# Where a decoder step's output copies are issued: three sequences' cache copies of each layer leave the search stage

## The chip, the cores and the metric

One core of a Trainium2 chip runs the whole kernel as one program. The metric is device time in microseconds (us) for one execution; lower is better. The engines that appear are TensorE (PE in the rows, its weight loads PEld), the vector engine (DVE), the scalar engine (ACT), GpSimd (POOL) and SyncE (SP). SyncE and GpSimd issue the transfers; all transfers run on the core's 16 DMA engines.

## The reference, cut to what matters

One inference step of a two-layer decoder trunk in float32: 256 prompt tokens and 8 sequences with 4 new tokens each, model width 1024.

```python
def layer_sample(x, pool_kv, pool_ki, layer, page_table, dil_bufs, conv_state, ssd_state, prm):
    (q_a, k_a, v_a, g_a, qi, ki, wi, q_c, k_c, v_c, g_c, z, xbc, dt_raw) = mixer_inputs(x, norm_w, w_in, pos)
    o_a = dsa_sample(q_a, k_a, v_a, qi, wi, ki, pool_kv, pool_ki, layer, page_table)
    o_c, new_bufs = dilated_sample(q_c, k_c, v_c, dil_bufs)
    y_b, conv_new, h_new = ssd_branch(z, xbc, dt_raw, conv_state, ssd_state, ...)
    y = x + merge_out(o_a, g_a, o_c, g_c, y_b, w_out)

def dilated_sample(q, k_new, v_new, bufs):
    for buf, kn, vn in zip(bufs, split_groups(k_new), split_groups(v_new)):
        kk = jnp.concatenate([buf[:, :, 0], kn], axis=1)
        vv = jnp.concatenate([buf[:, :, 1], vn], axis=1)
        new_bufs.append(jnp.stack([kk[:, t_new:], vv[:, t_new:]], axis=2))
```

A layer normalises x, multiplies it with one input matrix, runs three branches (sparse attention over 2048 cached tokens, of which the best 256 by an index score are kept for each query; dilated window attention with windows of 128, 512 and 2048 tokens; a state-space branch) and adds the output product to x. Part of the result are the window caches `new_bufs`: the old cache of each sequence and group, shifted by four tokens, with the new ones at the end. The shifted part is only copied, from one DRAM tensor to another.

## The kernel before, in words

**Tiles.** All activations lie with features on partitions and 288 tokens (256 + 32) in the free dimension. The input matrix is cut into 35 tiles of 128 columns (`proj0` to `proj34`), the output matrix into 8 (`out0` to `out7`). Every tile is 8 matmuls of 128x128 by 128x288 in float32 and needs one weight tile of [128, 8, 128] floats. TensorE's helper `mm` (L825) writes nearly every matmul, `turn` (L875) the transposes.

**Stages of a layer, in TensorE's order.** The front: proj0 to proj7. The page stage: 16 pairs of cache pages for index scores and key products, with proj8 to proj15 between them. The search stage: proj16 to proj26, one or three counting matmuls in each, because the vector engine finds each query's 256th score bit by bit (31 steps of compare at L1453, count on TensorE, settle at L1464 and L1466). Then window keys, masks, the softmax, and the value stage with proj27 to proj34, in which pages of values and windows are read. Last the output tiles: out0, out1 and out2 are begun with parts that are ready early and end close together; out3 to out7 follow whole. After out2 and each tile behind it comes one matmul with ones that sums the squares of the next norm.

**Weights.** The tile `w` has four slots (WSLOTS = 4). SyncE loads the weights of a tile into the slot of the tile four places before, once that tile's last matmul is done: `next_w(i)` waits for `filled(proj i)` or `filled(out m)` and calls `load_w` (issue L425). The order runs on from out7 of layer 0 to proj0 of layer 1.

**Pages.** `kv` has eight slots. RING lists 74 items a layer in the order of their use: 32 key pages, 8 + 8 windows and 32 groups of values. `consumed(items)` calls `after`, which issues the load of the item eight places later, SyncE the even ones and GpSimd the odd ones (`load_item`, issues L397 and L404); each waits until the slot has been read. So in the last value groups of layer 0 the first eight key pages of layer 1 are already loaded.

**Copies.** `keep(b, use)` makes GpSimd wait for `filled(use)`, and then issues three DRAM-to-DRAM copies for sequence b of layer L (L496), one for each group: (window - 4) rows of 256 floats. There are 16 calls. In both layers they stand in GpSimd's program after proj16, 17, 18, 19, 20, 21, 23 and 24:

```python
def keep(b, use):
    pool.wait_ge(filled(use), nth(L, use))
    for g in range(3):
        pool.dma_start(a[f"keep{g}"][ly, b], a[f"buf{g}"][ly, b, 4 * 256:]).then_inc(S["copied"], 16)
```

Nothing but GpSimd's very last instruction waits for `copied`.

**GpSimd's order in a layer.** The odd page loads of the page stage; a memset of `qcz`; the conv tails; copies, feature outputs (`feat`, L500), masked state inputs (`masked`, L518) and the placing of the window queries (L539, L543), mixed by hand in the search stage; the odd loads of windows and values, with the state output between; the value features; the last page loads; then waits for all outputs of the layer except the copies. Every wait holds up what stands behind it. SyncE's order is `next_w` and `consumed` alone, and one load of the old states after the page stage.

Of the kernel before, what the change touches and what calls it, by code (L numbers as in the profile page):

```python
# [57 lines left out]
def slot_of(i):  # L58

    first = max(f for f in SLOTS if f <= i)  # L60
    return SLOTS[first] + i - first
# [43 lines left out]
def ring_counts():  # L105

    used, landed, total, n = [], [], [0] * NKV, 0
    for at, (kind, i) in enumerate(RING):
        end = f"ks{i // 8}" if kind == "page" and i // 2 % 4 == 3 else {("window", NB - 1): "dk", ("window", 2 * NB - 1): "do",
                                                                           ("value", NGRP - 1): "so"}.get((kind, i))  # L110
        n += 0 if end else i % 2 if kind == "page" else 1
        used.append((end, None) if end else ("kv_used", n + 1 - i % 2 if kind == "page" else n))
        total[at % NKV] += 16 if kind == "window" else 64
        landed.append(total[at % NKV])
    return used, landed, total, n


USED, LANDED, LANDED_ALL, KV_USED = ring_counts()


def chunk_of(u):
# [88 lines left out]
def build(nc, a):  # L210

    plan, _ = bank_plan()
    with ExitStack() as ctx:
# [103 lines left out]
        def filled(use):  # L317
            return S[f"filled{plan[use][0]}"]
# [4 lines left out]
        def nth(layer, what, n=None):  # L323

            if n is None:
                what, n = f"filled{plan[what][0]}", plan[what][1] + 1
            return layer * PER[what] + n
# [15 lines left out]
        def C(name, lo=0, hi=None, rows=slice(0, P)):  # L343
            o, wd = _C[name]
            return const[rows, o + lo:o + (wd if hi is None else hi)]
# [9 lines left out]
        def ptile(i, lo=0, hi=T, rows=slice(0, P)):  # L355
            return pt[rows, slot_of(i), lo:hi]
# [30 lines left out]
        def load_item(engine, kind, layer, at):  # L387


            if layer or at >= NKV:  # L390
                what, n = USED[at - NKV]
                l = layer if at >= NKV else layer - 1
                engine.wait_ge(S[what] if n else filled(what), nth(l, what, n))
            s = at % NKV
            what, item = RING[at]
            if what == "window":
                engine.dma_start(kv[:, s, 0:9 * P], a["dil"][layer, item]).then_inc(S[f"kv_in{s}"], 16)  # L397
                return
            rec, entry = (KREC, 4 * item) if what == "page" else (VREC, 4 * (KITEMS + item))
            pages = nc.values_load_multi_w_load_instructions(  # L400
                ptab[0:1, entry:entry + 4], engines=[kind], min_val=0, max_val=N_POOL - 1,
                skip_runtime_bounds_check_because="a page table names pages of the pool")[1]
            for r, page in enumerate(pages):
                engine.dma_start(kv[:, s, r * rec:(r + 1) * rec],  # L404
                                 a["kk" if what == "page" else "vv"][bass.ds(page + layer * N_POOL, 1)].rearrange("o p n -> (o p) n")
                                 ).then_inc(S[f"kv_in{s}"], 16)

        def after(engine, kind, layer, item):


            at = PLACE[item] + NKV
            layer, at = (layer, at) if at < len(RING) else (layer + 1, at - len(RING))
            if layer < DEPTH and at % 2 == (kind == mybir.EngineType.Pool):
                load_item(engine, kind, layer, at)
# [67 lines left out]
        @block.gpsimd  # L482
        def _(pool):
            POOL = mybir.EngineType.Pool
            pool.wait_ge(S["ptab_in"], 16)
            for i, item in enumerate((1, 3, 5, 7)):
                pool.wait_ge(filled(f"proj{i}"), nth(0, f"proj{i}"))
                load_item(pool, POOL, 0, item)
            for L in range(DEPTH):
                ly = bass.ds(L, 1)  # L490
# [7 lines that stand above are left out]
                def feat(lo, hi, o, landed_out="feat_out"):  # L498

                    pool.dma_start(a["feat"][ly, :, o:o + hi - lo, :].rearrange("o p a n -> (o p) a n"),  # L500
                                   pt[:, slot_of(lo):slot_of(lo) + hi - lo, :]).then_inc(S[landed_out], 16)

                def consumed(*items):

                    for item in items:
                        after(pool, POOL, L, item)

                for u in range(NPAIR):
                    consumed(("page", 2 * u), ("page", 2 * u + 1))
                    if u == 3:  # L510
                        pool.memset(qcz, 0.0).then_inc(S["qcz_zero"], 1)
                pool.wait_ge(S["conved"], nth(L, "conved", NXBC))
                pool.dma_start(a["tails"][ly].rearrange("o p a n -> (o p) a n"), tails[:, :, :]).then_inc(S["tail_out"], 16)
                def masked(b):

                    if b >= 2:
                        pool.wait_ge(filled(f"ss{b - 2}"), nth(L, f"ss{b - 2}"))
                    pool.tensor_scalar(xwb[:, b % 2, :], xws[0:32, 2, :], C("bm", b, b + 1, slice(0, 32)), None,  # L518
                                       ALU.mult).then_inc(S["xwb_ready"], 1)

                keep(0, "proj16")
                pool.wait_ge(S["roped"], nth(L, "roped", 9))
                feat(KI, KI + 1, 0, "ki_out")
                feat(KA, KA + 2, 1)
                keep(1, "proj17")
                keep(2, "proj18")
                pool.wait_ge(S["xws_ready"], nth(L, "xws_ready", 1))
                masked(0)
                masked(1)
                keep(3, "proj19")  # L530
                keep(4, "proj20")
                keep(5, "proj21")
                pool.wait_ge(S["roped"], nth(L, "roped", 12))
                pool.wait_ge(S["qcz_zero"], nth(L, "qcz_zero", 1))
                for g in range(3):
                    for h2 in range(2):
                        q = ptile(QC + g, TP, T, half(h2)).rearrange("p (b q) -> p b q", q=NQ)
                        place = qcz[half(h2), :].rearrange("p (g b q n) -> p g b q n", g=3, b=NB, n=32)[:, g, :, :, QCZ0 + h2]
                        pool.tensor_copy(place, q).then_inc(S["qcz_ready"], 1)  # L539
                for g in range(3):  # L540
                    for h2 in range(2):
                        q = ptile(QC + g, TP, T, half(h2)).rearrange("p (b q) -> p b q", q=NQ)
                        pool.tensor_copy(qcbd[half(h2), g, :, h2:2 * NB:2], q.rearrange("p b q -> p q b")).then_inc(S["qcbd_ready"], 1)  # L543
                keep(6, "proj23")
                keep(7, "proj24")
                consumed(*RING[32:40])
                pool.wait_ge(S["roped"], nth(L, "roped", 15))
                feat(KC, KC + 3, 5)
                masked(2)
                masked(3)  # L550
                consumed(*RING[40:44])
                masked(4)
                masked(5)
                consumed(*RING[44:46])
                masked(6)
                masked(7)
                consumed(*RING[46:54])
                pool.wait_ge(drained(f"ss{NB - 1}"), nth(L, f"ss{NB - 1}"))
                pool.dma_start(a["s_ssd"][ly].rearrange("o p a n -> (o p) a n"), state[:, :, :]).then_inc(S["h_out"], 16)
                pool.dma_start(a["p_ssd"][ly].rearrange("o p n -> (o p) n"), hfin[:, :]).then_inc(S["h_out"], 16)  # L560
                consumed(*RING[54:66])
                pool.wait_ge(drained(f"proj{VA + 1}"), nth(L, f"proj{VA + 1}"))
                feat(VA, VA + 2, 3)
                feat(VC, VC + 3, 8)
                consumed(*RING[66:])
                for name in ("ki_out", "feat_out", "tail_out", "h_out"):
                    pool.wait_ge(S[name], nth(L, name, PER[name]))
            pool.wait_ge(S["copied"], DEPTH * PER["copied"])
# [1623 lines left out]
```

## Time and profile before

| what | us |
|---|---|
| median of 3 runs | 673.66 |
| lowest and highest of them | 668.64 and 677.35 |
| the profiled execution's own time | 673.8 |
| its span, first to last instruction | 672.1 |
| TensorE busy | 611.9 (91%) |
| vector engine busy | 377.8 (56%) |
| GpSimd busy | 224.0 (33%) |
| scalar engine busy | 168.1 (25%) |

The core's DMA engines moved 198.38 MB, a mean of 295 GB/s; a DRAM-to-DRAM copy is counted once in it. The stages in this execution: search of layer 0 from 112 to 202 us, its output tiles from 303 to 334 us, front of layer 1 to 367 us, its page stage to 427 us, its search to 524 us, its output tiles from 629 to 660 us. In the rows a busy digit is tenths of a slice; "to landing" is the time from a transfer's issue to its semaphore.

### The profile page before, as it was taken

The page shows a single profiled execution, that of the slowest core. Times are in us where ns is not written, and L with a number is a line of the kernel's source. Part 1 is how long each engine was busy: PE and PEld are TensorE (multiplying, and loading weights), DVE is VectorE, ACT ScalarE, POOL GpSimd, SP SyncE. Part 2 cuts the span into 40 slices and gives each one's busy share as a digit, 9 for nine tenths or more (in the row PEclk, how much of TensorE's full clock was granted, in tenths as well). Part 3 has the DMA queues.
Part 4 walks back from the last instruction along what each step waited for, and adds up shares of the span by engine and source line. Part 5 has one row for each costly group of instructions (what it writes and reads, how often), then busy time and mean ns, then how long its engine had stood idle before and what let it go on. Part 6 is the DMA issues. An engine that isn't in the chain of part 4 may idle for free.

```text
span 672.1 us, 13786 instructions
## 1 busy us (share of the span) xinstructions
PE 611.9 (91%) x4870; PEld 426.9 (64%) x4870; DVE 377.8 (56%) x1150; ACT 168.1 (25%) x405; POOL 224.0 (33%) x406
## 2 busy tenths in 40 slices
PE   5999998888899989999999999988888989789994
PEld 3766564665567665667776656566665867556772
DVE  3765565677569545443167475577756855343413
ACT  3024222121113312451101433212201151126211
POOL 0507530241206676451000664124120377642000
PEclk9999999898889998999999999999878999889998
DMA  7979999999968989996334999999997598996031
GB/s 294 308 274 356 368 369 413 417 358 331 353 236 262 314 305 369 366 329 234 110 121 134 323 368 369 402 413 355 349 394 265 181 333 287 374 357 214 10 118 70
DMA packets 67766, 198.38 MB, mean 295 GB/s; under 512 B 11537, under 2 KB 40370, under 8 KB 66418
## 3 DMA queue, kind: packets, MB, share of 16 engines
q1 hardware_dynamic: 49682, 99.99, 42.8%
q0 software_dynamic: 18016, 97.50, 40.3%
q8 instruction: 39, 0.64, 0.4%
q14 instruction: 29, 0.24, 0.1%
HBM read 189.30 MB, written 52.00 MB: 359 GB/s over the span
## 4 chain that ended last, share of the span: by engine, by line
PE 63%; DVE 15%; DMA 13%; ACT 4%; issue 2%; SPq 2%; DVEq 0%; ACTq 0%
PE bank L825 60%; DMA w<-in_w 5%; DMA kv<-in_vv 4%; DMA kv<-in_kk 4%; DVE hit L1453 3%; PE bank L875 3%; SPq L404 2%; DVE tb L1466 1%; DVE st L1955 1%; ACT srow L766 1%; ACT shared L663 1%; DVE tb L1464 1%; DMA x<-in_x 1%; DVE shared L1576 1%; ACT shared L680 1%
## 5 line engine op out<-in xcount | busy, mean ns | idle before, releaser
L825 PE MATMUL bank<-xn,w 128*128 128x288 f32 x1120 | 307.0, 429 | 0.7 <-DMA w<-in_w 0.7
L825 PEld LDWEIGHTS bank<-xn,w 128*128 128x128 f32 x1120 | 213.9, 198 | 74.9 <-issue 19.1
L404 POOL DMA_DIRECT2D kv<-in_vv x160 | 86.3, 539 | 96.9 <-PE bank L825 69.5
L404 POOL DMA_DIRECT2D kv<-in_kk x128 | 68.8, 538 | 144.5 <-issue 96.1
L616 ACT ACTIVATE pt<-bank 128x288 f32<-128x288 f32 x48 | 19.6, 409 | 243.4 <-PE bank L825 243.4
L825 PE MATMUL bank<-pt,w 128*128 128x288 f32 x256 | 64.9, 407 | 0.0
L825 PEld LDWEIGHTS bank<-pt,w 128*128 128x128 f32 x256 | 48.3, 190 | 13.6 <-issue 0.8
L496 POOL DMA_DIRECT2D out_keep<-in_buf x48 | 23.5, 495 | 85.1 <-PE bank L825 78.7
L1453 DVE TENSOR_SCALAR_CACHE_REDUCE hit<-sc,tb 128x516 bf16<-128x516 f32 x62 | 46.5, 750 | 2.2
L825 PE MATMUL bank<-kv,pt 128*32 128x256 f32 x512 | 37.5, 404 | 11.0 <-DMA kv<-in_vv 10.7
L1464 DVE TENSOR_SCALAR tb<-bank 128x1 int32<-128x1 f32 x62 | 9.5, 153 | 48.7 <-PE bank L825 48.5
L825 PE MATMUL bank<-kv,qz 128*32 128x256 f32 x512 | 34.3, 385 | 0.0
L2022 DVE TENSOR_TENSOR x<-x,bank 128x288 f32<-128x288 f32 x16 | 7.3, 455 | 43.6 <-PE bank L825 43.3
L825 PEld LDWEIGHTS bank<-cnt,seg 128*128 128x128 f16 x68 | 6.9, 103 | 38.8 <-issue 36.7
L825 PE MATMUL bank<-cnt,seg 128*128 128x1 f16 x68 | 11.2, 169 | 21.8 <-DVE hit L1453 21.1
L1426 DVE COPY tails<-cin 128x3 f32<-128x3 f32 x14 | 7.2, 512 | 41.0 <-ACT cin L614 38.9
L825 PEld LDWEIGHTS bank<-kv,pt 128*32 128x32 f32 x512 | 14.1, 112 | 22.5 <-DMA kv<-in_vv 9.5
L825 PE MATMUL bank<-kv,shared 128*32 128x128 f32 x768 | 26.8, 285 | 0.0
L825 PE MATMUL bank<-pt 64*128 64x128 f32 (+3 forms) x168 | 26.3, 334 | 0.0
L518 POOL TENSOR_SCALAR xwb<-xws,const 32x384 f32<-32x384 f32 x16 | 21.2, 1329 | 13.4 <-DVE xws L1716 7.7
L583 ACT ACTIVATE phased<-x 128x288 f32<-128x288 f32 x24 | 10.5, 442 | 60.0 <-DVE x L2022 57.1
L825 PEld LDWEIGHTS bank<-pt 64*128 64x128 f32 (+2 forms) x168 | 17.9, 183 | 10.6 <-issue 9.8
(238 smaller groups left out, 796.7 us busy)
## 6 DMA issues: line engine op xcount, KB each, us to landing
w<-in_w SPq DMA_DIRECT2D x86, 512.0 KB, 7.3
out_keep<-in_buf POOLq DMA_DIRECT2D x16, 2044.0 KB, 13.0
kv<-in_kk SPq DMA_DIRECT2D x128, 160.0 KB, 8.2
kv<-in_kk POOLq DMA_DIRECT2D x128, 160.0 KB, 5.8
kv<-in_vv POOLq DMA_DIRECT2D x160, 128.0 KB, 5.6
kv<-in_dil SPq DMA_DIRECT2D x24, 576.0 KB, 7.5
kv<-in_vv SPq DMA_DIRECT2D x96, 128.0 KB, 7.3
out_keep<-in_buf POOLq DMA_DIRECT2D x16, 508.0 KB, 8.5
```

The source lines that it names most:

```text
L404: engine.dma_start(kv[:, s, r * rec:(r + 1) * rec], a["kk" if what == "page" else "vv"][bass.ds(page + layer * N_POOL, 1)].rearrange("o p ...
L496: pool.dma_start(a[f"keep{g}"][ly, b], a[f"buf{g}"][ly, b, 4 * 256:]).then_inc(S["copied"], 16)
L518: pool.tensor_scalar(xwb[:, b % 2, :], xws[0:32, 2, :], C("bm", b, b + 1, slice(0, 32)), None, ALU.mult).then_inc(S["xwb_ready"], 1)
L583: act.activation(squares[:, k % 2, 0:T], x[:, k, :], ACT.Square).then_inc(S["sq_ready"], 1)
L616: act.activation(ptile(i), src[:, 0:T], fn).then_inc(use, 1)
L663: act.activation(psa[:, i, 0:nk], psa[:, i, 0:nk], ACT.Exp, bias=st8[:, 1, i:i + 1], accum_out=st8[:, 2, i:i + 1]).then_inc(S["pexp"] if i ...
L825: return pe.matmul(out, lhsT, rhs, start=start, stop=stop, skip_group_check=True, **k)
L875: return pe.transpose(out, in_, ident(n))
L1426: dve.tensor_copy(tails[:, n, 0:3], cin[:, n % 2, TP:TP + 3]).then_inc(chain.next(), 1)
L1453: ts_(hit[:, :], sc[:, :], old.bitcast(F32), 0.0, ALU.is_ge, ALU.add, accum_out=cnt[:, 0:1]).then_inc(S["cnt_ready"], 1)
L1464: ts_(tb[:, 2:3], src[:, 0:1], float(TOPK_S), float(bit), ALU.is_lt, ALU.mult).then_inc(drained(f"count{n}"), 1)
L2022: tt_(x[:, m, :], x[:, m, :], src[:, 0:T], ALU.add).then_inc(drained(f"out{m}"), 1)
```

## The change

Before, the calls stood one by one in GpSimd's program; now three tables say which sequence is copied where. The search stage keeps five calls a layer, after proj16, 17, 19, 21 and 23. In layer 0 they carry sequences 0 to 4, and sequences 5, 6 and 7 are copied after out0, out3 and out6. In layer 1 sequences 0 and 1 are copied after proj1 and proj5, ahead of the page loads in GpSimd's program, sequences 2 to 6 in the search stage, and sequence 7 after out0. The number of copies, their sizes and their destinations stay. No other engine's program changes.

```diff
@@ -116,6 +116,11 @@
 
 
 USED, LANDED, LANDED_ALL, KV_USED = ring_counts()
+
+
+FRONT_KEEPS = ((), ((0, "proj1"), (1, "proj5")))
+STAGE_KEEPS = ((0, 1, 2, 3, 4), (2, 3, 4, 5, 6))
+OUTPUT_KEEPS = (((5, "out0"), (6, "out3"), (7, "out6")), ((7, "out0"),))
 
 
 def chunk_of(u):
@@ -505,6 +510,8 @@
                     for item in items:
                         after(pool, POOL, L, item)
 
+                for b, use in FRONT_KEEPS[L]:
+                    keep(b, use)
                 for u in range(NPAIR):
                     consumed(("page", 2 * u), ("page", 2 * u + 1))
                     if u == 3:
@@ -518,18 +525,16 @@
                     pool.tensor_scalar(xwb[:, b % 2, :], xws[0:32, 2, :], C("bm", b, b + 1, slice(0, 32)), None,
                                        ALU.mult).then_inc(S["xwb_ready"], 1)
 
-                keep(0, "proj16")
+                keep(STAGE_KEEPS[L][0], "proj16")
                 pool.wait_ge(S["roped"], nth(L, "roped", 9))
                 feat(KI, KI + 1, 0, "ki_out")
                 feat(KA, KA + 2, 1)
-                keep(1, "proj17")
-                keep(2, "proj18")
+                keep(STAGE_KEEPS[L][1], "proj17")
                 pool.wait_ge(S["xws_ready"], nth(L, "xws_ready", 1))
                 masked(0)
                 masked(1)
-                keep(3, "proj19")
-                keep(4, "proj20")
-                keep(5, "proj21")
+                keep(STAGE_KEEPS[L][2], "proj19")
+                keep(STAGE_KEEPS[L][3], "proj21")
                 pool.wait_ge(S["roped"], nth(L, "roped", 12))
                 pool.wait_ge(S["qcz_zero"], nth(L, "qcz_zero", 1))
                 for g in range(3):
@@ -541,8 +546,7 @@
                     for h2 in range(2):
                         q = ptile(QC + g, TP, T, half(h2)).rearrange("p (b q) -> p b q", q=NQ)
                         pool.tensor_copy(qcbd[half(h2), g, :, h2:2 * NB:2], q.rearrange("p b q -> p q b")).then_inc(S["qcbd_ready"], 1)
-                keep(6, "proj23")
-                keep(7, "proj24")
+                keep(STAGE_KEEPS[L][4], "proj23")
                 consumed(*RING[32:40])
                 pool.wait_ge(S["roped"], nth(L, "roped", 15))
                 feat(KC, KC + 3, 5)
@@ -563,6 +567,8 @@
                 feat(VA, VA + 2, 3)
                 feat(VC, VC + 3, 8)
                 consumed(*RING[66:])
+                for b, use in OUTPUT_KEEPS[L]:
+                    keep(b, use)
                 for name in ("ki_out", "feat_out", "tail_out", "h_out"):
                     pool.wait_ge(S[name], nth(L, name, PER[name]))
             pool.wait_ge(S["copied"], DEPTH * PER["copied"])
```

## Rows read from the trace of the kernel before

**Rows 1.** The page's 40 slices of 16.8 us, whole run.

```profile
PE   5999998888899989999999999988888989789994
...
DMA  7979999999968989996334999999997598996031
```

**Rows 2.** Waits of PE: engine, line, released by: us, times, longest.

```profile
PE bank L825 <- DVE hit L1453: 21.1, 20, 1.7
PE bank L825 <- DMA kv<-in_vv: 10.7, 8, 2.6
...
PE bank L825 <- DMA w<-in_w: 0.7, 1, 0.7
```

**Rows 3.** Stretches: us, busy time by engine, PEclk, DMA share, GB/s.

```profile
112.00:202.00 90.00, 78.91 (x430) 55.63 (x425) 60.65 (x229) 15.29 (x45) 18.27 (x40) 0.91 0.93 343
303.00:322.00 19.00, 19.00 (x92) 14.72 (x91) 5.78 (x17) 2.21 (x6) 1.32 (x3) 1.00 0.58 202
322.00:359.00 37.00, 37.00 (x154) 28.74 (x153) 19.40 (x49) 4.49 (x10) 0.00 (x0) 1.00 0.39 128
```

**Rows 4.** DMA issues: form, count, KB each, median us to landing.

```profile
w<-in_w SPq DMA_DIRECT2D x86, 512.0 KB, 7.3
out_keep<-in_buf POOLq DMA_DIRECT2D x16, 2044.0 KB, 13.0
...
out_keep<-in_buf POOLq DMA_DIRECT2D x16, 508.0 KB, 8.5
...
out_keep<-in_buf POOLq DMA_DIRECT2D x16, 124.0 KB, 6.7
```

**Rows 5.** GpSimd's copies: issue time in ns, span of starts, landing.

```profile
L496 POOL DMA_DIRECT2D out_keep<-in_buf x48: 486/497/532, 117.7 to 505.9; - x48
...
DMA to landing us min/median/max: 4.7/10.9/24.5
```

**Rows 6.** Landing of proj24's weights: layer 0 (issued 147.1), then layer 1.

```profile
DMA to landing us min/median/max: 23.9/23.9/23.9
...
L425 SPq DMA_DIRECT2D w<-in_w x1: 328/328/328, 467.9 to 467.9; - x1
...
DMA to landing us min/median/max: 30.9/30.9/30.9
```

**Rows 7.** DMA queues in 475:485: packets, MB, share.

```profile
q0 software_dynamic: 116, 3.00, 83.4%
q1 hardware_dynamic: 115, 0.41, 13.5%
```

**Rows 8.** Weight loads issued in 310:313, layer 0's output tiles.

```profile
L425 SPq DMA_DIRECT2D w<-in_w x3: 328/338/339, 310.5 to 312.4; - x3
...
DMA to landing us min/median/max: 3.4/5.7/6.0
```

**Rows 9.** Timeline of PE in 317:331: start, us, tile's matmuls.

```profile
317.07 4.04 PE L825 MATMUL bank<-pt,w 128*128 128x288 f32 x16
...
321.43 4.04 PE L825 MATMUL bank<-pt,w 128*128 128x288 f32 x16
...
325.80 4.04 PE L825 MATMUL bank<-pt,w 128*128 128x288 f32 x16
```

**Rows 10.** Landing of GpSimd's first value load, issued at 205.9.

```profile
DMA to landing us min/median/max: 2.5/2.7/2.9
```

**Rows 11.** Stretches in which PE waited for value pages.

```profile
249.00:254.00 5.00, 1.87 (x38) 1.17 (x40) 0.00 (x0) 0.00 (x0) 4.37 (x9) 0.85 1.01 344
...
575.00:580.00 5.00, 2.94 (x44) 1.78 (x40) 0.00 (x0) 0.00 (x0) 3.40 (x7) 0.68 1.07 401
```

**Rows 12.** Weight loads issued in 636:640, layer 1's output tiles.

```profile
L425 SPq DMA_DIRECT2D w<-in_w x3: 328/328/339, 636.7 to 638.7; - x3
```

**Rows 13.** Weight loads in 343:359.2; SyncE's first page load of layer 1.

```profile
L425 SPq DMA_DIRECT2D w<-in_w x5: 328/328/328, 343.4 to 359.0; - x5
...
370.27 0.88 SPq L404 DMA_DIRECT2D kv<-in_kk  x2
```

## The prediction

> **What bounds the kernel now.** I read the slices first [rows 1]: TensorE is at 8 or 9 tenths almost everywhere, and the DMA row is also at 9 except in two hollows, slices 20 to 23 (from the end of layer 0 into the front of layer 1) and the last four. So the matmuls set the time, and the transfers are close behind. Then TensorE's waits [rows 2]: 21.1 us for the vector engine's hits in the search, 10.7 us for value pages, and for weights one wait of 0.7 us in the whole run. Then the stretches that the change touches [rows 3]: the search stage of layer 0 (112 to 202 us) has a DMA share of 0.93 and a granted clock of 0.91; the output tiles and the next front (303 to 359 us) have 0.58 and 0.39, and TensorE is busy for all 56 us. The search therefore has little DMA time left and TensorE is often idle there; the output stretch has much DMA time left and TensorE never idle. What is moved is 3 of 8 copies per layer from the first to the second.
>
> **What one copy weighs.** keep(b) issues three DRAM-to-DRAM copies of 2044, 508 and 124 KB [rows 4], 2676 KB or 2.74 MB. A weight tile is 512 KB, 0.524 MB [rows 4]. All 48 are issued between 117.7 and 505.9 us, 0.5 us of GpSimd each, and take 4.7 to 24.5 us to land [rows 5].
>
> **Part 1: search stage, copies taken out.** The issue costs GpSimd 1.5 us a copy. The whole of it lies in GpSimd's own waits; nothing on TensorE's path reads it. The visible price of the copies is the late weight tile. The one issued at 467.9 us needs 30.9 us to land [rows 6]; it is the cause of the 0.7 us wait of [rows 2]. By the code six copies stand around it, one after each of proj16 to proj21, each 2.74 MB or some 8 us of DMA, and the tile is proj24's. With five copies spread over proj16, 17, 19, 21 and 23 the pile is gone: gain 0.7 us. Bounds: 0, and 5 us if the loads are later in other executions than in this one; I take 0.7, what the row shows. The vector engine's waits and the clock of 0.91 come from the search's chain, which no copy feeds, so I count nothing there. The copy after proj24 disappears, but the value loads begin only once the search is over, at 205.9 us, and land in 2.5 to 2.9 us [rows 10], on idle DMA, so it gives nothing. The other transfers of GpSimd in the stage (features, masks, the query copies) keep their order and their later waits.
>
> **Part 2: how a weight load fares beside a copy.** In 475 to 485 us only copies and weight loads move [rows 7]: queue 0 (GpSimd's) passed 116 packets with 3.00 MB, queue 1 (SyncE's) 115 packets with 0.41 MB. They alternate packet for packet, and a copy's packets are seven times as large. One weight tile is 0.524 MB, so beside a copy it takes 0.524/0.041, about 12.8 us; alone it takes 3.4 us [rows 8]. In the search nobody minds: 11 projections share 90 us, some 8 us each, and four slots give about 30. An output tile lasts 4.04 us plus the norm's matmul, 4.37 us from one to the next [rows 9], and four slots are gone in 13.
>
> The Trainium skill ("DMA: Bandwidth & Descriptors", SWDGE vs HWDGE vs iDMA) says the engine changes queue at packet borders and that a packet is preferably at most 4096 B. Equal packets would share the bandwidth evenly and no weight would be late. The trace shows 3.6 KB a packet on SyncE's queue and 26 KB on GpSimd's, so for these copies I go by the row; the page's case is rival B.
>
> **Part 3: layer 0, copies after out0, out3 and out6.** out0 ends at 310.5 us and out3 at 316.8 us, because the first three output tiles end almost together (weights are requested at 310.5, 311.4 and 312.4) [rows 8]. So copy 5 and copy 6 start only 6.3 us apart, and each needs 2.74/0.36 = 7.6 us alone: they run back to back. Walk through the weights:
> - out4's tile is requested at 310.5 us, at the same moment as copy 5. It lands after 3.4 us and is needed at 317.1 [rows 8, 9]. GpSimd's transfers land at the earliest 2.5 us after issue [rows 10], so the copy begins when most of the tile has passed: 0, bounds 0 to 3 us.
> - out5's tile (needed at 321.4) and out6's (needed at 325.8) queue behind it, beside both copies. From 311.6 us, when the tile starts, two copies and three tiles must pass: 2 x 2.74 + 3 x 0.524 = 7.05 MB. At 0.369 MB/us (343 GB/s at a share of 0.93 [rows 3]) that ends at 330.7 us, at 0.341 MB/us [rows 7] at 332.3 us. Three tiles have more packets than two copies, so the last tile is the last to land: out6 starts at 331 to 332.3, 5.2 to 6.5 us late. I take 5.8. Bounds: 0 (the tiles pass first) and 10 (out4's tile is caught behind a large packet and out5's then waits for both copies).
> - After TensorE idles for 2 to 3 us in 5, the clock is granted at 0.68 and 0.85 of full [rows 11]. At 0.68, 64% of the 5 us are at 1.2 GHz: 1.6 us lost. I add 1.6 us once; bounds 0 and 3.2.
> - copy 7 after out6 is alone. The tile requested with it is ahead of it, the next is 12 us under way and needed after 17. Nothing.
>
> **Part 4: layer 1, copies after proj1 and proj5.** proj1 ends at 343.4 us, proj5 at 359.0 [rows 13]; the copies are 15.6 us apart, so each is alone, and by the same walk each tile is in time by 3 us or more. GpSimd waits for proj1 and proj5 with its page loads queued behind, but their slots are freed by the first page pair; SyncE's first is issued at 370.3 us [rows 13]. At the start of the front it has nothing else to do. Copy 1, issued at 359, ends near 371 us; the first page load after it fills a slot of an eight-slot ring whose other six slots, three pairs of some 3.7 us, are still to be read (16 pairs lie in the 60 us from 367 to 427), so it is needed near 381. Cost 0, bounds 0 to 2 us.
>
> **Part 5: layer 1, copy 7 after out0.** Three tiles are requested between 636.7 and 638.7 us [rows 12]. One copy and two tiles are 3.79 MB, 10.3 us from 637.9: 648.2 us, and out5 wants its tile 10.9 us after out0's end, as in layer 0, at 647.6. I take 1 us with the completion, bounds 0 and 3. GpSimd's last wait, for all copies, ends near 650, with 22 us to the end as cover.
>
> **Sum.** On the profiled execution, 673.8 us around a span of 672.1 and beside a median of 673.66: minus 0.7, plus 5.8, plus 1.6, plus 1.0 is plus 7.7, **681.5 us**.
>
> **Rivals.**
> A is the forecast: two copies back to back hold up the output weights of layer 0. 678 to 686 us, chance 0.50.
> B: the weights pass. SyncE's descriptors might be ready earlier than GpSimd's, and the share packet for packet may hold only while both queues are full. For it: the tile of 310.5 us lands before the copy starts. Against it: [rows 7]. 673.8 - 0.7 = 673.1 us; with one small wait, 675. Chance 0.27.
> C: more of it. out4's tile is caught by a large packet in both layers, and out5's waits behind both copies: 10 + 3.2 (two clock drops) + 3 (layer 1) + 1 (front) - 0.7 = 16.5, 690 us. Chance 0.13.
> D, on the other side: the late weights of the search are the main thing. In layer 0 the same tile took 23.9 us, in layer 1 30.9 [rows 6]; TensorE can stand about 30. An execution with a slightly slower DMA pays that lateness on each tile of the pile, 4 to 5 us, and the executions shown go from 668.64 to 677.35. If removing it gives 5 us and the output stretch costs nothing, 669 us. It decides where more than two tiles of the search are late; here one is. Chance 0.10.
> That GpSimd reaches the new places late, and the copies are not moved at all in effect, I exclude: behind its last page loads for layer 1, which wait for the value groups and not for an output tile, nothing keeps it from those waits.
>
> **Range and chances.** Two per cent, 13.5 us, is about what a measurement of this kernel can tell from no change. Below 660.2 us lies only an unknown cause: 0.02. Above 687.1 lies C: 0.13. Within: 0.85. The range of 670 to 688 us holds A and B whole and leaves out half of D and most of C. A alone has 678 to 686.
>
> **What would show it.** Right: a wait of TensorE for weights of 5 to 7 us between 317 and 333 us, out6's first matmul near 331.5, weight loads of 10 to 18 us to landing there against 3.4 to 6.0, a slice with a clock below 1.0 in the output tiles, and in the search weight loads below 20 us with no wait. Wrong: no wait for weights there (B); a first matmul of out4 after 318 us (C); a search stage shorter by more than 2 us (D). A longer page stage in layer 1 would break part 4.

## The result, and the profile after

| | before | after |
|---|---|---|
| median of the runs, us | 674.07 (4 runs) | 686.97 (4 runs) |
| lowest and highest | 668.64 and 677.35 | 685.61 and 688.84 |
| the profiled execution's span | 672.1 | 685.7 |

The change makes the kernel slower: the ratio is 1.0202, with a 95% interval of 1.0151 to 1.0253. The forecast was 681.5 us, plus 7.7; it came to plus 12.9. Here and below the medians hold every run, while a ratio and its interval leave out the runs more than 1.5% above the fastest of the same kernel.

The page of the changed kernel, in 40 slices of 17.1 us; the first and third line answer to [rows 1]:

```profile
PE   5999998989999979997999989988889998899974
...
PEclk9999999999899989999999999999988999899998
DMA  7879999976639899999798999999751788994331
```

The DMA row's hollow after layer 0 is filled, and new ones lie in the search of layer 0 (slices 10 to 12) and of layer 1 (slices 29 to 31). PE's 7 in slice 19 (309 to 326 us) is new, and so is the 7 in slice 39 (651 to 669 us). In those two slices and just behind them lies most of the loss. TensorE's waits, which answer to [rows 2]:

```profile
PE bank L831 <- DVE hit L1459: 19.7, 20, 1.7
PE bank L831 <- DMA kv<-in_vv: 10.8, 7, 2.5
PE bank L831 <- DMA w<-in_w: 9.3, 3, 4.0
...
PE bank L831 <- DMA kv<-in_kk: 4.2, 5, 1.5
```

The vector engine's and the value pages' waits are as before (19.7 against 21.1, and 10.8 against 10.7). The weights have gone from 0.7 to 9.3 us in three waits, and the key pages from 2.6 to 4.2. All weight waits stand in output tiles. The three loads requested after out0, out1 and out2 of layer 0, where [rows 8] had 3.4 to 6.0 us:

```profile
L430 SPq DMA_DIRECT2D w<-in_w x3: 328/339/339, 310.0 to 311.9; - x3
...
  PE bank L831: 5.5, 2
...
DMA to landing us min/median/max: 3.6/14.1/21.0
```

The middle line says what TensorE waited for them. In the timeline of PE, which answers to [rows 9], out4, out5 and the beginning of out6:

```profile
316.58 4.04 PE L831 MATMUL bank<-pt,w 128*128 128x288 f32 x16
...
325.09 5.84 PE L831 MATMUL bank<-pt,w 128*128 128x288 f32 x16 [3.98 <-DMA w<-in_w]
...
332.95 4.15 PE L831 MATMUL bank<-pt,w 128*128 128x288 f32 x16 [1.53 <-DMA w<-in_w]
```

out4 starts as before. out5's weights come at 325.1 us, 14.1 us after their request, and out6's at 332.9, after 21.0. The forecast had out4 on time and out6 between 331 and 332.3. out5 is also slower in itself, 5.84 us against 4.04. The stretches behind the two long waits, with the granted clock in the third column from the end, answer to [rows 11]:

```profile
322.00:326.00 4.00, 0.91 (x3) 0.72 (x4) 0.00 (x0) 0.00 (x0) 0.00 (x0) 0.95 1.13 359
326.00:330.00 4.00, 4.00 (x11) 2.90 (x11) 0.00 (x0) 0.00 (x0) 0.00 (x0) 0.63 0.82 290
655.00:660.00 5.00, 1.23 (x6) 0.67 (x5) 0.46 (x1) 0.44 (x1) 0.00 (x0) 1.00 0.67 240
660.00:665.00 5.00, 5.00 (x16) 3.60 (x15) 0.00 (x0) 0.00 (x0) 0.00 (x0) 0.66 0.02 9
```

After TensorE worked 0.91 of 4 us, the clock is granted at 0.63 in the next 4; after 1.23 of 5 us in layer 1, at 0.66. That is the second price beside the wait itself: out5's matmuls run mostly at 1.2 GHz and take 1.8 us longer. In layer 0 it isn't paid on top, because out6's weights come only at 332.9 us, after out5 has ended. In layer 1 out6's weights are there in time, and it is paid. The tiles requested in layer 1 after out1 and out2, where copy 7 starts with out0:

```profile
L430 SPq DMA_DIRECT2D w<-in_w x2: 328/328/328, 645.6 to 646.5; - x2
...
  PE bank L831: 3.8, 1
...
DMA to landing us min/median/max: 13.9/14.0/14.2
```

Where the 13.6 us between the two spans came from follows from five marks in both timelines (first and last addition to x of a layer's outputs, the new keys' dots that open the page stage, the scores that close it, the selection of value sums ahead of the outputs):

| stretch | before | after | difference |
|---|---|---|---|
| start to the first output of layer 0 | 310.5 | 310.0 | -0.5 |
| output tiles of layer 0 and front of layer 1 | 57.5 | 65.3 | +7.8 |
| page stage of layer 1 | 67.0 | 68.4 | +1.4 |
| search and value stage of layer 1 | 194.3 | 193.4 | -0.9 |
| output tiles of layer 1, to the last addition | 31.2 | 37.0 | +5.8 |
| the rest | 11.6 | 11.6 | 0.0 |

How far each line can be trusted is seen from the same marks in the profiles of the experiments below. Wherever no weights were late, the second line is 57.5 or 57.6 us and the fifth 31.2 or 31.3, so +7.8 and +5.8 are the change's. The first line goes from 306.2 to 316.6 us and the fourth from 187.8 to 194.6 without any order by placement, so -0.5 and -0.9 say nothing.

In the search the copies' going did what was said of it, and no more: layer 1's weight loads there landed in 5.6 to 30.9 us before; now it is

```profile
L430 SPq DMA_DIRECT2D w<-in_w x10: 327/328/912, 448.6 to 523.0; - x10
...
DMA to landing us min/median/max: 3.4/4.5/13.1
```

and no wait for them is left. The search stretch of layer 0, which answers to the first line of [rows 3]:

```profile
112.00:202.00 90.00, 80.25 (x486) 56.86 (x486) 62.90 (x234) 16.59 (x47) 13.93 (x31) 0.92 0.71 260
```

The DMA share is 0.71 in place of 0.93, the clock 0.92 in place of 0.91. From its scores to the first maximum of the softmax the search of layer 0 took 96.2 us against 99.1, and that of layer 1 99.3 against 99.9. The 2.9 us in layer 0 look like the sign that the prediction gave for rival D, but they go with the clock of that execution (last section) and not with the copies: experiment 2, which leaves layer 0's copies where they were, has 97.7 us there. What was freed there was of no use that can be shown.

### The profile page after: what moved, and what is told of

Read it like the earlier page. It is cut to its first block, busy times and chain, and to the rows that moved or that the text cites. A ratio compares the mean times of both kernels' runs of the same rounds, so it can differ in the third digit from the quotient of the medians.

```text
span 685.7 us, 13786 instructions
## 1 busy us (share of the span) xinstructions
PE 617.2 (90%) x4870; PEld 429.8 (63%) x4870; DVE 376.7 (55%) x1150; ACT 168.4 (25%) x405; POOL 224.3 (33%) x406
## 2 busy tenths in 40 slices
DMA packets 67766, 198.38 MB, mean 289 GB/s; under 512 B 11537, under 2 KB 40370, under 8 KB 66418
## 3 DMA queue, kind: packets, MB, share of 16 engines
q0 software_dynamic: 18016, 97.50, 39.4%
## 4 chain that ended last, share of the span: by engine, by line
PE 59%; DVE 16%; DMA 16%; ACT 4%; issue 3%; SPq 2%; DVEq 0%; ACTq 0%
PE bank L831 56%; DMA kv<-in_kk 6%; DMA w<-in_w 5%; DMA kv<-in_vv 4%; DVE hit L1459 4%; PE bank L881 3%; SPq L409 2%; DVE tb L1472 1%; DVE tb L1470 1%; DVE st L1961 1%; ACT srow L772 1%; ACT shared L669 1%; DMA x<-in_x 1%; DVE shared L1582 1%; ACT shared L686 1%
## 5 line engine op out<-in xcount | busy, mean ns | idle before, releaser
L831 PE MATMUL bank<-pt,w 128*128 128x288 f32 x256 | 68.6, 424 | 9.3 <-DMA w<-in_w 9.3
L831 PEld LDWEIGHTS bank<-pt,w 128*128 128x128 f32 x256 | 50.2, 199 | 25.2 <-DMA w<-in_w 10.7
L831 PE MATMUL bank<-kv,pt 128*32 128x256 f32 x512 | 37.1, 400 | 11.1 <-DMA kv<-in_vv 10.8
L831 PE MATMUL bank<-cnt,seg 128*128 128x1 f16 x68 | 11.2, 169 | 20.4 <-DVE hit L1459 19.7
L589 ACT ACTIVATE phased<-x 128x288 f32<-128x288 f32 x24 | 10.5, 442 | 73.8 <-DVE x L2028 70.6
```

The lines of the kernel that those rows point to most:

```text
L589: act.activation(squares[:, k % 2, 0:T], x[:, k, :], ACT.Square).then_inc(S["sq_ready"], 1)
L831: return pe.matmul(out, lhsT, rhs, start=start, stop=stop, skip_group_check=True, **k)
```

## The experiments

Each kernel was timed against the kernel before on the same chip; "before" below is that comparison's own median. The edits are given against the kernel before, shortened to what they do. `stage_keep(use)` issues the copy that a table names for this place, and none where the table has no entry.

**1. Layer 0's part alone.**

```diff
+STAGE_KEEPS layer 0: proj16, 17, 19, 21, 23 -> sequences 0 to 4
+OUTPUT_KEEPS layer 0: (5, "out0"), (6, "out3"), (7, "out6")
 layer 1: as before
```

> Layer 0 as in the change (copies after proj16, 17, 19, 21, 23 and after out0, out3, out6), layer 1 as before. Theory 1 (two copies back to back take the DMA time of the weights of out5 and out6): TensorE waits for weights 5 to 6 us in layer 0's output tiles, out5's matmuls run partly at the lower clock, and nothing else changes: 6 to 8 us above before, 680 to 682 us. Rival (the copies in the front and after layer 1's out0 cost the most, or the whole program is shifted by something general): under 3 us above before.

Measured: 683.38 us against 672.99, ratio 1.0154 (1.0072 to 1.0237). The mechanism is there, the median is larger than expected (four runs; the interval reaches from 4.8 to 16 us). The timeline of PE, out4, out5 and out6:

```profile
318.54 4.04 PE L839 MATMUL bank<-pt,w 128*128 128x288 f32 x16
...
329.43 5.53 PE L839 MATMUL bank<-pt,w 128*128 128x288 f32 x16 [6.36 <-DMA w<-in_w]
...
335.28 4.04 PE L839 MATMUL bank<-pt,w 128*128 128x288 f32 x16
```

Here out5's weights come 6.4 us late and out6 then finds its own in place. This is another order of the same walk: out5's tile lands at 329.4 us, 5.4 us after the first copy's large part and 4.2 us before the second's. The forecast's upper bound (10 us) was for out5 behind both copies. The stretch of output tiles and next front took 65.5 us, 8.0 more than before, so the order hardly changes the price. The profile has another 3.1 us of waits for weights in the search of layer 1, whose copies stand at the old places (loads there landed in up to 36.1 us, and the waits were 2.7 and 0.4 us). That belongs to the kernel before as well, which had 0.7 us of it in its own profile.

**2. The front alone.** Sequences 0 and 1 of layer 1.

```diff
+FRONT_KEEPS layer 1: (0, "proj1"), (1, "proj5")
-keep(0, "proj16"), keep(1, "proj17") in layer 1
```

> Only layer 1's copies 0 and 1 are moved, to proj1 and proj5 of its front; all else as before. Theory 1 (single copies with a tile's distance around them cost nothing in the front): 0 to 2 us above before, all of it in the page stage behind the copy at proj5. Rival (each moved copy costs the same, 13 us over 6 copies): 4 to 5 us above before.

Measured: 673.4 us against 672.99, ratio 1.0029 (0.9982 to 1.0076). Copies with a tile's distance to the requests cost little. The interval, up to 5.1 us, doesn't quite exclude the rival of an equal price for each copy (4 to 5 us); the profile does: output tiles and front took 57.6 us against 57.5, the page stage behind them 67.9 against 67.0. There seems to be a small price: the page stage of layer 1 takes 67.9, 68.4, 68.5, 69.1 and 69.4 us in the five kernels that issue a copy after proj5, and 66.4 to 67.7 in the eight that don't. These are single executions. Layer 0's page stage, which no copy precedes in any kernel, takes 67.0 to 67.9 us in twelve of them and 71.8 in experiment 11, whose 69.4 is therefore a weak witness. About 1 us is what is left. The changed kernel's last part of that copy, 2044 KB:

```profile
L501 POOL DMA_DIRECT2D out_keep<-in_buf x1: 497/497/497, 368.9 to 368.9; - x1
...
DMA to landing us min/median/max: 11.1/11.1/11.1
```

GpSimd issues it at 368.9, 2.4 us behind the copy's first part, and it lands at 380.0. That is 13.5 us after the first issue, where I had 12. The pages that GpSimd loads from 378 us on are behind it.

**3. Layer 1's copy 7 alone.**

```diff
+OUTPUT_KEEPS layer 1: (7, "out0")
-keep(7, "proj24") in layer 1
```

> Only layer 1's copy 7 is moved, to out0; all else as before. Theory 1 (the tile of out5 waits behind the one copy, then the clock drops): one wait for weights of 3.5 to 4.5 us and 1.8 us of slower matmuls, 5 to 6 us above before. Rival (the wait in the changed kernel came from its late start or from chance): under 2 us.

Measured: 677.37 us against 672.99, ratio 1.0072 (1.0035 to 1.0108). The weight loads after out0, out1 and out2 of layer 1:

```profile
L430 SPq DMA_DIRECT2D w<-in_w x3: 328/328/338, 636.3 to 638.2; - x3
...
  PE bank L839: 1.4, 1
...
DMA to landing us min/median/max: 3.7/11.5/13.5
```

The profiled execution had a wait of 1.4 us, less than the changed kernel's 3.8, no slower tile behind it, and output tiles 1.7 us longer than before; the ten timed ones lose 4.4 in the median. The 3.5 to 4.5 us of waiting and 1.8 us of slower matmuls that I expected are not in this profile. So one copy has a price of its own, and it varies.

**4. Rows of 4096 bytes, the first attempt.**

```diff
-pool.dma_start(new, old)
+for lo, hi in ((0, n - n % 16), (n - n % 16, n)):     # n rows of 4096 bytes
+    pool.dma_start(new rows lo:hi as [rows, 1024], old rows lo:hi as [rows, 1024])
```

> All copies where the change puts them, but each is issued as rows of 4096 bytes (a part with a multiple of 16 rows and the rest of it), so that the packets of both queues are alike; twice as many issues on GpSimd. Theory 1 (a weight load is late because the DMA engines alternate packet for packet and a copy's packets are many times larger): weight loads land in 4 to 8 us beside a copy, no wait for weights over 1 us, 672 to 676 us. Rival (a copy's bytes alone fill the DMA, whatever their packets): waits for weights of 9 us as in the changed kernel, 685 to 688 us.

Measured: 677.61 us against 672.99, ratio 1.011 (1.0008 to 1.0212). The page's count of packets, and two of the issue groups:

```profile
DMA packets 69304, 198.39 MB, mean 293 GB/s; under 512 B 12306, under 2 KB 41139, under 8 KB 67955
...
out_keep<-in_buf POOLq DMA_DIRECT2D x16, 1984.0 KB, 9.4
...
out_keep<-in_buf POOLq DMA_DIRECT2D x48, 60.0 KB, 6.4
```

This is a miss as a test. The kernel before has 67766 packets, this one 69304, 1536 of them from GpSimd's queue. The kernel before issues 48 parts and this one 96, so each further issue brought 32 packets, 16 of them below 512 bytes (12306 against 11537). Rows of 4096 bytes would be over 600 packets a copy: rows that lie one behind the other were joined to long packets again. What had changed is only when the parts are issued. GpSimd paused after the second of the six issues and began the 1984 KB part about 3.7 us after the first part (the changed kernel's large part starts after 1.0 us), out5 and out6 had their weights in time, and two waits of 1.4 and 1.0 us came in the front, a third of 1.0 us in layer 1's output tiles. That pointed to the moment of the large packets as the thing to test, besides their size.

**5 and 6. Rows of 4096 bytes, 8192 apart.** The large parts go as two interleaved sets of rows, which can't be joined; in 5 at the places of the change, in 6 at those of before.

```diff
+for t in range(2):                                    # the first 480 (or 96) rows
+    pool.dma_start(rows t, t + 2, t + 4, ... of new, the same rows of old)
+pool.dma_start(the rest of new, the rest of old)
```

> All copies where the change puts them, but the large parts are issued as two interleaved sets of rows of 4096 bytes, rows 8192 bytes apart, so that a packet can't hold more than one row (contiguous rows had been joined again in the kernel before this one). Theory 1 (alternating packet for packet with large packets makes the weights late): the two queues' packets are alike, weight loads land in 4 to 8 us beside a copy, no wait for weights over 1 us, 672 to 675 us. Rival (the copy's bytes fill the DMA, whatever the packets): 9 us of waits as in the changed kernel, 684 us and more.

Measured: 675.25 us against 672.63, ratio 1.0047 (1.0008 to 1.0086). No wait for weights is left. The loads after out0, out1 and out2 of layer 0, and the two queues from 312 to 322 us, beside copy 5:

```profile
L430 SPq DMA_DIRECT2D w<-in_w x3: 328/338/338, 309.2 to 311.2; - x3
...
DMA to landing us min/median/max: 3.5/7.9/10.0
```

```profile
q0 software_dynamic: 455, 1.64, 50.8%
q1 hardware_dynamic: 389, 1.45, 41.0%
```

In the changed kernel the same stretch, 313 to 323 us, has

```profile
q0 software_dynamic: 147, 3.32, 87.3%
q1 hardware_dynamic: 161, 0.61, 16.5%
```

The bytes of a copy are the same, and a load beside it takes 7.9 to 10.0 us in place of 14.1 to 21.0. Where both queues are full and the packets alike (3.6 KB and 3.7 KB), they share 455 to 389. So the size of the packets, not the bytes, made the weights late, and the rival falls. One thing differs besides: with seven issues a copy, the large rows start 2.5 us after out4's request and not 1.2. That can't make the two queues share alike once both are at work, but it may be part of why no wait is left. 2.6 us are left; the page stage of layer 1 has 1.5 of them (68.5 us against 67.0).

> The kernel before with the same rows of 4096 bytes in its copies. Theory 1: the weight loads of the search stage land in under 12 us in place of 10 to 31, the one wait of 0.7 us is gone, and nothing else gains: 670 to 674 us, no difference from before. Rival (the late weights of the search cost several us in most executions): 668 us or less. Small packets might also make the copies themselves longer; if they spill into the value loads, 675 us and more.

Measured: 673.55 us against 672.63, ratio 1.0021 (0.998 to 1.0062). The search's weight loads land in 6.4 to 9.1 us in layer 1, where they had 5.6 to 30.9, and it gains nothing: the late weights of the search cost nothing that the medians can show. Here the copies start where they did before, so the shorter landing is the packets' doing.

**7. Output copies after out3 and out6.**

```diff
+STAGE_KEEPS layer 0: proj16, 17, 18, 19, 21 -> 0 to 4, proj23 -> 7
+OUTPUT_KEEPS layer 0: (5, "out3"), (6, "out6")
```

> Layer 0's copies 5 and 6 after out3 and out6, copy 7 back in the search after proj23 and copy 5's old place left empty; layer 1 as before. Theory 1 (out0 is the bad place, because out4, out5 and out6 are requested within 2 us there and a second copy follows before the first is done): no wait for weights, or one under 1.5 us, 672 to 676 us. Rival (any copy between output tiles makes weights late): 4 us or more for each of the two, 681 us and more.

Measured: 673.4 us against 672.63, ratio 1.0026 (0.9978 to 1.0073), and no wait for weights; output tiles and front take 57.5 us, as before. Two copies in the output tiles, with weights landing in 9.7 and 9.3 us beside them, cost nothing that shows when the requests are 4.4 us apart and the copies 13 (the interval reaches up to 4.9 us).

**8. No copies.**

```diff
-pool.dma_start(a[f"keep{g}"][ly, b], a[f"buf{g}"][ly, b, 4 * 256:]).then_inc(S["copied"], 16)
```

> The kernel before without its 48 copies; the shifted part of the window caches isn't written. It bounds what any placement can give. Theory 1 (the search stage pays 0.7 us for its copies): 671 to 673 us, the search stages no more than 1 us shorter. Rival (the copies slow the search by several us through late weights or otherwise): 667 us or less, with both search stages shorter by 2 us or more.

Measured: 674.07 us against 672.63, ratio 0.9995 (0.9954 to 1.0035). The search of layer 0 and the weight loads of layer 1's:

```profile
112.00:202.00 90.00, 78.87 (x426) 55.12 (x423) 59.37 (x224) 16.00 (x45) 6.63 (x16) 0.91 0.29 103
```

```profile
L430 SPq DMA_DIRECT2D w<-in_w x11: 327/328/328, 438.2 to 518.6; - x11
...
DMA to landing us min/median/max: 3.3/3.5/7.0
```

With a third of its DMA share (0.29 for 0.93) and weights in 3.5 us, TensorE is busy for 78.87 us of the 90, before it was 78.91, and the search of layer 0 took 99.3 us against 99.1 at the same clock of 0.91. In the old places the copies were free within the interval's 0.5%, some 3 us, so no placement of them could have won more than that. The kernel without copies also leaves out the last wait, for `copied`.

**9. One copy after out0 in layer 0.**

```diff
+STAGE_KEEPS layer 0: proj16, 17, 18, 19, 21, 23 -> 0, 1, 6, 2, 3, 4
+OUTPUT_KEEPS layer 0: (5, "out0"), (7, "out6")
```

> Layer 0's copies 5 and 7 after out0 and out6, copy 6 back in the search (after proj18); layer 1 as before. Against a_l0_outputs it takes away the second of the two copies that follow each other. Theory 1 (out5's and out6's weights wait for both copies): the weights wait only behind one, so 1.5 to 4 us of waits and up to 1.8 us for the clock: 675 to 678 us, half of a_l0_outputs' loss or less. Rival (the loss comes from one copy after out0, the second adds nothing): 680 us and more.

Measured: median 678.58 us against 673.75, ratio 1.0031 (0.9989 to 1.0073), but the ten runs go from 670.26 to 685.45. As a size this is inconclusive. The profiled execution, with 680.42 us one of the long ones, is read for its order alone: one wait, for out5, and out6 finds its weights:

```profile
319.10 4.04 PE L839 MATMUL bank<-pt,w 128*128 128x288 f32 x16
...
326.90 4.15 PE L839 MATMUL bank<-pt,w 128*128 128x288 f32 x16 [3.27 <-DMA w<-in_w]
```

out5's tile takes 4.15 us after this wait, and 1.00 is granted in 326 to 331 us: the lower clock didn't follow here.

**10. Layer 1's copy 7, 1.9 us later.**

```diff
+OUTPUT_KEEPS layer 1: (7, "out2")
```

> As c_l1_out0, but layer 1's copy 7 starts after out2 in place of out0, 1.9 us later, when the weights of out4, out5 and out6 are all requested. Theory 1 (what counts is how many packets of the weights are ahead of the copy's): out5's tile is through before the copy's large packets come, no wait for weights over 0.5 us, within 1.5 us of before. Rival (a copy anywhere in the output tiles costs the same): 4 us above before, as c_l1_out0.

Measured: 672.63 us against 673.75, ratio 0.998 (0.9942 to 1.0017); against experiment 3 the whole loss is gone. The copy's issue and the three weight loads:

```profile
633.87 1.49 POOL L501 DMA_DIRECT2D out_keep<-in_buf  x3 [23.21 <-PE bank L839]
```

```profile
L430 SPq DMA_DIRECT2D w<-in_w x3: 327/328/338, 631.7 to 633.6; - x3
...
DMA to landing us min/median/max: 3.5/4.6/5.9
```

The three loads are requested from 631.7 to 633.6 us, the copy at 633.9. They land in 3.5 to 5.9 us, as in [rows 8].

**11. The change, shifted.**

```diff
+STAGE_KEEPS layer 0: proj16, 17, 18, 19, 21 -> 0 to 4, proj23 -> 7; layer 1: as in the change
+OUTPUT_KEEPS: layer 0 (5, "out2"), (6, "out5"); layer 1 (7, "out2")
+FRONT_KEEPS layer 1: (0, "proj1"), (1, "proj5")
```

> The change with its output copies shifted: layer 0's copies 5 and 6 after out2 and out5 (13 us apart), its copy 7 left in the search after proj23, layer 1's copies 0 and 1 after proj1 and proj5 as in the change, its copy 7 after out2. Theory 1 (the loss is the moment of the copies against the weight requests, not their place in the output and front stretches): no wait for weights over 1 us in any output tile, 672 to 676 us, 11 us or more below the change. Rival (five copies outside the search cost what the change costs, wherever they start): 681 us and more. Since the kernel without any copies isn't faster than before, neither theory has it below 671 in the median.

Measured: 675.94 us against 672.31, ratio 1.0069 (1.0033 to 1.0105). No wait for weights; TensorE's waits for pages:

```profile
PE bank L839 <- DMA kv<-in_vv: 10.2, 6, 3.0
...
PE bank L839 <- DMA kv<-in_kk: 5.5, 3, 2.7
```

The median is 11 us below the change's, and the loss against the kernel before on the same chip went from 12.9 to 3.6 us, by moving three starts by 2 to 9 us and leaving one copy in the search. Output tiles and front are back at 57.5 us, and layer 1's output tiles at 31.2. Of the 3.6 us some 1 us may be the copy after proj5 (experiment 2); for the rest there is no run. The rows above don't name it: 3.3 of the 5.5 us for key pages lie in layer 0's page stage, ahead of every copy.

## Why the prediction was right or wrong

**What bounds the kernel, and part 1.** Right. The stall of 0.7 us went, nothing else did that can be told from the spread. One reading was careless: the hollow of the DMA row is slices 19 to 22, and slices 12, 31 and 32 are low as well (6, 7 and 5); nothing in the sum uses it. The bound of 5 us that I kept for part 1 (rival D) is refuted by experiments 6 and 8: without late weights, and even without copies, the median stays. Single executions can pay more than 0.7, as the 3.1 us in experiment 1's profile show. The executions of before differ by 9 us for another reason, below.

**Part 2, the alternation.** Right in what it does, shown by experiment 5 against the changed kernel. The page of the Trainium skill ("DMA: Bandwidth & Descriptors", SWDGE vs HWDGE vs iDMA) gives 4096 bytes as the packet that is preferred; with such packets its case (rival B) is what happens, no late weights. The copies as written have other packets, and the trace of before had said so. [rows 7] had 116 packets against 115; the changed kernel has 147 against 161 in 313 to 323 us, and with alike packets it is 455 to 389.

**Part 3, layer 0.** Right in the mechanism; that the sum fits so well is partly luck. Forecast 5.8 + 1.6 = 7.4 us, measured 7.8 in the profile; out4 in time, out6 at 332.95. But out6 alone started 7.65 us late (22.95 us after out0's end in place of 15.3), and the slower matmuls of out5, which I had added on top, passed while out6's weights were still under way. So one term was 1.9 us too small and the other cost nothing extra. The walk had three tiles beside the two copies, 7.05 MB; from 311.6 to 332.9 us 7.62 MB passed, since the tiles requested after out3 and out4 were in the queue too. The order of out5 and out6 is not fixed: in experiment 1 out5 had the whole wait. There the stretch lost 8.0 us, so either order costs about the same.

**Part 4, the front.** Nearly right: no late weights in the front, but 1.4 us in the page stage, where I had 0 with a bound of 2. Copy 1 was issued 7.5 us later than in my walk, because of layer 0's loss, and took 13.5 us in place of 12. I had left out that GpSimd's issue can itself be held up, here by 1.4 us between two parts (by what, the profile doesn't show), and the large part took 11.1 us to land from its own issue.

**Part 5, layer 1's copy 7.** This is the term that failed, by its size. I took 1.0 us (bound 3); it measured 5.8 in the profile, and in experiment 3, where it stands alone, 4.4 in the median (2.4 to 7.3) and 1.7 in the profile. Two things were missing. The first is bytes. The tile of out5 landed 13.9 us after its request, when I had 10.5. I let one copy and two tiles pass, 3.79 MB. From 645.8 us to 659.5, when the tile landed, the two queues passed

```profile
q0 software_dynamic: 112, 2.74, 51.8%
q1 hardware_dynamic: 537, 1.96, 39.2%
```

which is the copy and nearly four tiles: out4's, of which 0.04 MB had passed before, and out7's, requested at 650.9 us, are in it. They passed at 344 GB/s, where I had 369 at a full share; most of the error is the 0.9 MB. How little of the weights gets through beside the copy's large part is plainest in 650 to 655 us, packet for packet:

```profile
q0 software_dynamic: 27, 1.50, 74.3%
q1 hardware_dynamic: 28, 0.10, 5.0%
```

The second is the clock. I charged it only in layer 0, though a like wait is followed by it in layer 1: 1.8 us of the 5.8.

In the profile the steps add up so: forecast 7.7, measured 13.6. Part 5 is 4.8 of the difference, part 4 is 1.4, part 3 is 0.4, and the other stretches gave 1.4 where the forecast had 0.7 for the search, which is within their spread. The medians differ by 12.9. **Rival C** (690 us) is nearer to the time, but its first cause, out4's weights caught in both layers, is in none of the profiles; its second, out5 behind both copies, is in experiment 1's in part, at 8.0 us where C had 13.2 with its two drops of the clock. In the changed kernel the time came from layer 1 instead.

## What to carry to other kernels

Before moving a transfer out of a busy stage, ask what it costs there: run the kernel without it. Here it cost nothing that could be measured: a DMA share of 0.93 didn't slow the stage. And count every request that falls into the stretch, those made while it lasts too. A transfer with large packets should start after the small requests with the nearest deadline are under way, not together with them; in layer 1, 1.9 us decided over 4 us (experiments 3 and 10).

## What the runs showed that was not expected

The spread of the kernel before goes with the granted clock, not with the copies. Over the executions of all kernels without late weights, a mean clock of 0.969 or 0.970 stands beside 666 to 671 us and one of 0.955 to 0.957 beside 671 to 681. The kernel without copies took 666.26 us at 0.970 and 674.9 at 0.960. The profiles show one place where it arises, the search of either layer. In the thirteen profiles it took 98.5 to 99.9 us where 0.91 was granted in it, and 94.6 to 94.8 where 0.95 was; at 0.93 it took 96.2 to 97.7, and 98.3 once with 3.1 us of waits for weights in it. The search of layer 0 without copies is among the longest (99.3 at 0.91). What makes the clock differ from one execution to the next, and whether it is the cause of the longer search or goes along with it, was not tried.

Rows that lie one behind another are joined into long packets, though the program writes them as rows of 4096 bytes: 1536 packets more, 32 for each of the 48 more issues (experiment 4). A gap between the rows keeps them apart (experiment 5: 28000 packets on GpSimd's queue in place of 18016).
